# A hybrid DeltaNet and sparse-attention layer on one core: projection pieces through all of the last scan, own PSUM banks for the scan, split convolutions, and a new order of the attention's memory scores and norms

## The reference, cut to what matters

```
h = x @ w_in                              # 1024 rows, split into the groups below
A: qkv = silu(short_conv(q_a, k_a, v_a))  # 4 taps; 4 heads x 128
   per head, chunks of 64 tokens: U, W = solve(I + lower(KB KT), [VB, KB exp g])
   scan over the chunks: v_new = U_i - W_i S;  o_i = Q_i S + A_i v_new;  S = S g_i + K_i^T v_new
   o_a = rmsnorm(o) * silu(z_a)
B: score[q, s] = sum_j relu(qi_j . ki_s) * wi_j;  the 256 largest keys per query are kept
   attention of 4 heads over a shared latent of 128 with these keys, ALiBi bias;  * silu(z_s)
C: softmax(q_m . k_m) v_m over 256 memory tokens, 4 heads of 64;  * silu(z_m)
y = concat(o_a, o_s, o_m) @ w_out
out = LayerNorm(alpha * x + y)
```

## Time and profile before

| what | us |
|---|---|
| median of 3 runs | 781.16 (780.77 to 781.71) |
| the profiled execution | 782.2 |
| its span | 780.4 |
| TensorE (PE) busy | 712.9, 91% of the span |
| VectorE (DVE) busy | 483.9, 62% |
| ScalarE (ACT) busy | 452.2, 58% |
| GpSimd (POOL) busy | 181.7, 23% |
| PE busy from 470 to 515 | 44.22 of 45 |
| PE busy from 515 to 552 | 30.50 of 37 |
| PE busy from 552 to 600 | 35.51 of 48 |
| PE busy from 600 to 765 | 150.31 of 165 |

### The profile page before, as it was taken

One profiled execution on the slowest core, in us unless ns is written; L12 is line 12 of the kernel. 1 busy time (PEld: TensorE's weight loads), 2 busy tenths in 40 slices (PEclk: granted clock), 3 DMA queues, 4 the chain that ended last, 5 costly groups with the idle time before them and its releaser, 6 DMA issues.

```text
span 780.4 us, 11927 instructions
## 1 busy us (share of the span) xinstructions
PE 712.9 (91%) x4204; PEld 591.0 (76%) x4204; DVE 483.9 (62%) x1076; ACT 452.2 (58%) x1027; POOL 181.7 (23%) x272
## 2 busy tenths in 40 slices
PE   6999999989999999999999989998777989899994
PEld 4887888778788888887888778876566767686773
DVE  5532888966756757563755658686644465654643
ACT  5522777787869987799959962223752242423410
POOL 0000000045102621136102431010365343143330
PEclk9999999999999999999999999999978999999998
DMA  9411020122300340023300252010961231332101
GB/s 356 133 68 63 19 95 29 40 72 63 120 28 29 92 136 28 28 72 89 122 28 28 85 142 83 28 47 33 333 181 40 75 115 47 109 97 74 68 28 55
DMA packets 63915, 65.90 MB, mean 84 GB/s; under 512 B 16368, under 2 KB 49392, under 8 KB 63472
## 3 DMA queue, kind: packets, MB, share of 16 engines
q1 hardware_dynamic: 63856, 65.13, 25.7%
HBM read 48.35 MB, written 16.78 MB: 83 GB/s over the span
## 4 chain that ended last, share of the span: by engine, by line
PE 63%; DVE 13%; ACT 11%; issue 9%; POOL 2%; DMA 2%; SPq 0%; ACTq 0%; DVEq 0%; POOLq 0%
PE bank L1054 10%; PE bank L1056 10%; PE bank L1055 10%; ACT cst L1938 4%; PE bank L1046 4%; PE bank L1408 4%; PE bank L1060 3%; PE bank L1409 3%; PE bank L1410 3%; DVE score L1534 2%; PE bank L1350 2%; PE bank L1240 2%; PE bank L1238 2%; PE bank L1219 2%; POOL w_out_lo L2194 2%
## 5 line engine op out<-in xcount | busy, mean ns | idle before, releaser
L1054 PE MATMUL bank<-x_hi,ring_split 128*128 128x512 f32 x480 | 197.1, 411 | 8.3 <-DVE x_lo L1483 7.3
L1056 PE MATMUL bank<-x_hi,ring_split 128*128 128x512 f32 x480 | 188.4, 393 | 0.0
L1055 PE MATMUL bank<-x_lo,ring_split 128*128 128x512 f32 x480 | 187.9, 392 | 0.0
L1938 ACT ACTIVATE cst<-score,sel 128x896 bf16<-128x896 f32 (+3 forms) x192 | 167.1, 873 | 25.7 <-DVE sel L1556 23.6
L1054 PEld LDWEIGHTS bank<-x_hi,ring_split 128*128 128x128 f32 x480 | 90.8, 189 | 25.3 <-DVE ring_split L1487 7.8
L1056 PEld LDWEIGHTS bank<-x_hi,ring_split 128*128 128x128 f32 x480 | 90.5, 189 | 19.8
L1055 PEld LDWEIGHTS bank<-x_lo,ring_split 128*128 128x128 f32 x480 | 90.9, 189 | 15.0
L1855 ACT ACTIVATE arena<-bank 128x512 f32<-128x512 f32 (+1 forms) x69 | 37.4, 563 | 55.7 <-PE bank L1060 48.6
L2125 POOL TENSOR_TENSOR arena<-arena,hsc 128x512 f32<-128x512 f32 x8 | 8.3, 1039 | 259.4 <-ACT arena L2008 259.4
L1408 PE MATMUL bank<-w_out_hi,mix_hi 128*128 128x512 f32 x128 | 54.4, 425 | 11.4 <-DVE mix_lo L1801 7.8
L2112 POOL TENSOR_TENSOR arena<-arena,cst 128x512 f32<-128x512 f32 x24 | 33.3, 1409 | 92.9 <-PE bank L1219 50.3
(11 more groups left out here) (288 smaller groups left out, 1400.9 us busy)
## 6 DMA issues: line engine op xcount, KB each, us to landing
ring<-in_w_groups SPq DMA_DIRECT2D x30, 512.0 KB, 3.4
x_raw<-in_x_t SPq DMA_DIRECT2D x8, 512.0 KB, 9.3
side_z<-stage SPq DMA_DIRECT2D x16, 256.0 KB, 2.0
w_out_sb<-in_wout_t SPq DMA_DIRECT2D x2, 2048.0 KB, 11.5
zgT<-side_z SPq DMA_DIRECT2D x8, 512.0 KB, 4.5
qkvT<-in_x SPq DMA_DIRECT2D x8, 512.0 KB, 3.4
out_y<-arena SPq DMA_DIRECT2D x8, 512.0 KB, 3.0
ring<-in_wmem_t SPq DMA_DIRECT2D x2, 1024.0 KB, 4.7
```

The lines of the kernel that those rows point to most:

```text
L1054: nc.tensor.matmul(dst, hi, xh, start=(c == 0), stop=False)
L1055: nc.tensor.matmul(dst, hi, xl, start=False, stop=False)
L1056: last = nc.tensor.matmul(dst, lo, xh, start=False, stop=(c == KT - 1))
L1938: sc.activation(signs[order[e] % 2][:, 0:w], score[:, score_at(b):score_at(b + 1)], ACT.Sign, scale=-1.0, bias=candidate[:, b - 2:b - 1], ...
```

## The change

Eight edits, all but the second and the last in the plan:

1. The last scan has side pieces through all eight steps, as the other scans have projection pieces; the four scores of the first attention block (b = 3) stand behind the scan.
2. `scanV` always takes bank 4, the state of `scanS` bank 5, the scan's outputs banks 6 and 7 in turn. Before, all three took turns in banks 4 to 7.
3. Each `conv` step on DVE (four taps) is cut into two steps of two taps, the second one or more units later in the list.
4. In the start of head 0 the transposes `KBT` stand one unit later, the product `U` two units later, `latent_scale` and `base` behind them; the number of units stays.
5. `norms` of a block stands right before its `memory`, not among the transposes.
6. `msc` of the next block stands one score earlier (from the third block on).
7. In the second half of a block's output `mixT` and `mix_split` stand side by side, with the empty units behind them.
8. The score step's maximum waits for the exponentials of the block before; `wait_ge(exps_ready, ...)`.

```diff
-N_LAST_FILLED = 5
...
         if part < 2:
-            units[3].append(("conv", h, part, 0))
-            units[7].append(("conv", h, part, 1))
+            units[3].append(("conv", h, part, 0, 0))
+            units[4].append(("conv", h, part, 0, 1))
+            units[7].append(("conv", h, part, 1, 0))
+        if part == 0:
+            units[0].append(("conv", h, 1, 1, 1))
...
-    ahead = [*pair("GB", 0), 1, ("KB", 0, 0), ("KB", 0, 1), 1, 1, *pair("KBT", 0), 1, 1, *product(0), *[1] * 5, ("latent_scale",), ("base", 0), *[1] * 6, ("diag_back", 0), 2]
+    ahead = [*pair("GB", 0), 1, ("KB", 0, 0), ("KB", 0, 1), 1, 1, 1, *pair("KBT", 0), 1, 1, 1, *product(0), *[1] * 4, ("latent_scale",), ("base", 0), *[1] * 5, ("diag_back", 0), 2]
...
-            if more or b < N_LAST_FILLED:
-                if not more:
+            if not more:
+                if b < 5:
                     steps += [[("values", 3), ("q_first",), ("kh", 0, 1)], [], [("kh", 1, 0)], [("kh", 1, 1)], [("values", 2), ("qsplit", first_block), ("qsplit", BLOCK_ORDER[1])]][b]
-                steps += [("scanV", h, b), 1.2, ("scanS", h, b), 1]
-            else:
-                n = b - N_LAST_FILLED
-                steps += [("scanV", h, b), *scores(first_block, n), ("scanS", h, b), *(scores(first_block, 3) if b == NB - 1 else [])]
+            steps += [("scanV", h, b), 1.2, ("scanS", h, b), 1]
...
-        units[min(5, len(units) - 1)].append(("norms", b))
...
         pieces = [[("y", b, c, s0 + s)] for c in range(2) for s in range(2)]
+        if i:
+            return [[("mixT", b, i), ("mix_split", b, i)], [], [], [], [], *pieces]
         return [[("mixT", b, i)], [("mix_split", b, i)], [], [], *pieces]
...
+    for h in range(SAH):
+        for e in scores(first_block, h):
+            add(e)
...
-            place = 3 if n else 4
+            place = 2 if n else 4
             at[place:place] = [[("msc", nb, 0), ("msc", nb, 1)]]
...
+        add(("norms", b))
         add(("memory", b))
...
-        return [("D", ("V", e[1], e[2]))]
+        return [("V", ("V", e[1], e[2]))]
     if k == "scanS":
-        return [("D", ("S", e[1], e[2]))] * (e[2] < NB - 1) + [("D", ("O", e[1], e[2]))]
+        return [("S", ("S", e[1], e[2]))] * (e[2] < NB - 1) + [("R", ("O", e[1], e[2]))]
...
-        pools = {"P": (0, 1), "L": (2, 3), "D": (4, 5, 6, 7), "A": (4, 5, 6), "O": (0,), "Y": (1, 7)}
+        pools = {"P": (0, 1), "L": (2, 3), "D": (4, 5, 6, 7), "V": (4,), "S": (5,), "R": (6, 7), "A": (4, 5, 6), "O": (0,), "Y": (1, 7)}
```

29 lines of the change are left out of this document (16 added, 13 removed).

## The result

The changed kernel takes 788.71 us in the median of 8 runs (783.38 to 790.41); the kernel before, on the same chips, 781.95 us (780.77 to 783.77, 8 runs). The ratio is 1.0074 (95% interval 1.0055 to 1.0093). The difference of the medians is 6.8 us. I had forecast 774.2, with a range of 768 to 781: the sign is wrong.

A forecast was written before the change was run, and what follows sets the result against it. TensorE, busy 91% of the span, bounds the kernel; gains come only from its 67 us idle or its clock. -4.0 + 5.0 - 8.0 = -7.0 us on 782.2 gives 775.2, less 1.04 for the median: 774.2 us, range 768 to 781.

The forecast's parts named there:

- the wait of the norms: At the turn to the attention, TensorE's 2.4 us wait for the norms goes (would be -1.7), but gains nothing.
- Start of head 0: Transposes of KB and product U: more cover recovers 2.2 us of 4.2, bounds 0.5 and 3.5.
- Convolutions: At 215.1 us TensorE's 0.71 us wait for DVE behind a four-tap convolution goes: gain 0.9 us, bounds 0 and 0.9.
- Banks: scanV's waits for `o_head`, heads 0 to 2: fixed banks gain 0.9 us of 4.3, bounds 0 and 4.3.
- The front's sum: Start of head 0, convolutions and banks together, up to head 3: -4.0 us, range used -1.5 to -5.5.
- Last scan: Head 3's scan: waits in steps 5 to 7 go (2.2 us), but 2.2 us comes back; no gain of its own.
- Turn: From last scan to attention: the later last side store delays SP's queue and `mixT` of block 3: +5.0 us, bounds +1 and +13.
- rival (c): Turn: late queries and late o_head add up and the clock falls; +13 us there, 782 to 786 in all; chance 0.11.
- Attention: 600 to 765 us: bank waits of 9.1 us, 10.7 with restarts, mostly go: -8.0 us, bounds -4 and -11.
- three quarters: Attention: the share taken as gain from seven bank waits, 10.7 us with restarts, giving -8.0 us.
- (a): Front and attention: bank waits only move to another name; -1.5 us in all, some 779 to 780; chance 0.17.
- my 0.10: Whole kernel: the chance given to the change being slower, by over 0.2%.

The follow-up runs named there:

- first profile: Profiled execution of the changed kernel, all eight edits, in its first set of runs: 783.38 us, the fastest of eight.
- second profile: The changed kernel run once more, unaltered, for another profile: one execution of 790.44 us.
- the front alone: Kernel before with only edits 3 and 4 (convolutions in halves, later start of head 0): 781.12 us against 782.37, ratio 0.9991.
- the experiment: Kernel before with edit 1 and one side piece moved from ahead of the last scan to between step 0's state and step 1's scanV: 784.96 us.

## Why the prediction was wrong, point by point

The forecast was -7.0 us and the medians say +6.8, so 13.8 us are to be found. By the medians of the single runs 2.9 are in front and banks (-4.0 forecast, -1.1 measured), 1.7 in edit 1 (+5.0, +6.7), 3.9 in the attention (-8.0, -4.1), and 5.3 in the addition itself: the terms were added up, and they do not add (3.2 us by the ratios). That last step has no line of its own in the prediction, and it may be the largest. The prediction had its reason written down, "since SP's chain decides there it gains nothing", but used it for the wait of the norms alone and not for the other gains.

- **Start of head 0, -2.2 us.** Right by name and place, too large in size: the 3.7 us of waits fell to 0.6 us, with a new one of 0.4. The first profile is at -2.1 us at `tok` of head 0, but 0.8 us of this was there at 23 us, before any edit acts. The second profile has -1.2, the front alone -1.1, so the gain is some 1.3 us and the agreement with 2.2 is luck. Then 1.0 us is given back at the next transposes, which wait 2.0 us for DVE (1.1 before), and the clock behind them fell to 0.70 in a stretch. The step "gain 2.2" failed: I followed the gain only to the next wait of the same steps, and not to the next place where TensorE meets DVE.
- **Convolutions, -0.9 us.** The wait at 215.1 is gone, as forecast. The row names no releaser ("issue"), so that it was DVE's convolution was a guess, which the result bears out.
- **Banks, -0.9 us of 4.3.** The reason was right (the state's update is directly ahead of the addition, so the wait moves to the second matmul), and against the waits view's 4.3 us the order of the two DVE rows decided well. What I left out is the pool of banks 4 to 7, from which the other DeltaNet steps still take their banks in turn: a product of head 2 now meets a bank of the outputs for 1.5 us. Net 0.
- **The front's sum, -4.0 us.** Measured -0.4 and 0.0 at head 3, -1.2 by the medians of the front alone. This is the first term that failed in order of time.
- **Last scan, nothing of its own.** I had seen both causes and priced them at 1.0 us for the cover and 1.2 for the low part, 2.2 in all. The wait they made is 2.6 us, so this is near. Its place was wrong: I had looked for it at `vnew` in step 0, which still waits 1.5 us as before, and it came at the state, in scanV of step 1. What failed is the term that was left out, the clock: by the experiment the place costs 4.1 us, of which the wait is 2.6. The waits for `o_head` in steps 5 to 7 went, as forecast (ahead of scanV of step 5, where I had a piece, there is none, and it has no wait even so).
- **Turn, +5.0 us.** The mechanism is right in each link: the late store (+8.0 us in the first profile, 6.7 forecast), the chain and the slack of 1.5 us. The size is 6.6 us in the first profile (from -0.4 at head 3 to +6.2 at mixT, the last scan included) and 8.5 in the second. From the last output of the scan to mixT alone it is 5.7 and 5.6 us, and 5.1 where the gap in step 1 is filled, so most of the excess is the last scan's. The time by which the queries are late is 5.0 us by the two places given (558.1 and 553.1), not 4.6; only rival (c) rests on it.
- **Attention, -8.0 us.** The waits named went, all of them (9.1 us), and edits 5 and 6 alone gave 4.9. The step that failed is "three quarters": I priced what the edits remove and not where DVE's list is then late. That is the last score of a block, 3.5 us, and with 0.7 us of smaller ones the 9.1 us become the 4.9 measured. For edit 7, counted at 0, it is the second score, 5.0 us: +3.9 alone, and between 0 and 1.0 us in company.
- **The rivals.** (a) "the bank waits only move" is what happened in front and attention. (c) had the right sign and an end, 786, near the result, but not for its reason: the late queries did not add up with the late `o_head`. In all eight profiles with a late last piece TensorE waits last for the scale (0.7 to 5.0 us), so the queries ran beside it, and from the last output to mixT the turn took 3.8 to 5.7 us more, not 13. I had given each rival its chance as if the other parts came out as forecast. With the front at 0, the turn at +7 and the attention at -4 the sum is +3, so slower was likelier than my 0.10.
- **The rules that were cited.** The rule of the Trainium skill, "TensorE: Matmul & The Clock Gate", section "HAM oscillation — how this bites in real kernels", that gaps between bursts bring the clock down, is borne out by the rows at 520 and 672, though not by every gap: of 17 profiles, all with a wait of 1.8 to 1.9 us at the transposes of head 3, two have a low clock behind it. I cited it and put 1.9 us for it into one rival only. That of the Trainium skill, "PSUM — Partial Sum Buffer", section "Engine vs sequencer instructions", strict order in DVE's queue, agrees with all the successors: `dn_s`, `misc` at the second and `misc` at the last score.

## What to carry to other kernels

When independent pieces are spread over dependent steps, look first at which steps stand side by side with no piece between them, and price such a place by what the other engine has queued there; one piece in its right place, with the low part that moved behind the state by it, was worth 4.1 us here, and the last one in its old place 3.7 us, because a queue of transfers stood behind its store. The place at step 5, where DVE had nothing queued, cost nothing. A wait for a bank that an in-order engine releases is seldom removed by another bank or an earlier step: look for the next thing that this engine is late for, and count that against the gain. Gains between the start of a fixed chain and the place where it arrives late are lost, so edits are to be timed alone and in company. And compare a profile with its own runs first: a lead that is there before any edit acts belongs to the execution.

## What was not expected of the hardware

The kernel before varies by 3 us between executions (780.77 to 783.77), the changed one by 7 (783.38 to 790.41), edit 7 alone by 7 (782.86 to 789.80), and the change without edit 1 by 8 (773.24 to 781.41). The same wait at the same place is followed by the lower clock in one execution and not in another: the transposes of head 3, which wait 1.8 to 1.9 us in all 17 profiles, have 0.62 behind them in the second profile of the change and 0.64 in that of the change without edits 5 to 7, and 1.00 in the other fifteen, the first profile and the kernel before among them. The wait of 2.6 us in step 1 of the last scan was followed by a lower clock in all six profiles that have it (0.50 to 0.76 from 520 to 524). A single profile, if it is the fastest execution, as here, shows neither this nor the time.
